# Ten sums of squares: the halves of the columns added by VectorE, and one product with ones in place of two

## What is computed

```python
def rms_norm(x, w):
    xf = x.astype(jnp.float32)
    y = xf * lax.rsqrt(jnp.mean(xf * xf, axis=-1, keepdims=True) + EPS)
    return (y * w.astype(jnp.float32)).astype(x.dtype)
```

## Time and profile before

| | |
|---|---|
| time, median of 3 runs | 2177.81 us (2176.87 to 2178.8) |
| the profiled execution, its own time | 2178.8 us |
| its span, from the first to the last instruction | 2177.1 us |
| mean granted TensorE clock, as a share of full speed | 0.997 |
| busy: TensorE, VectorE, ScalarE, GpSimd | 98%, 53%, 33%, 54% of the span |

### The profile page before, as it was taken

One profiled execution on the slowest core, in us unless ns is written; L12 is line 12 of the kernel. 1 busy time (PEld: TensorE's weight loads), 2 busy tenths in 40 slices (PEclk: granted clock), 3 DMA queues, 4 the chain that ended last, 5 costly groups with the idle time before them and its releaser, 6 DMA issues.

```text
span 2177.1 us, 29202 instructions
## 1 busy us (share of the span) xinstructions
PE 2141.7 (98%) x11096; PEld 1742.0 (80%) x11096; DVE 1150.1 (53%) x1413; ACT 710.9 (33%) x878; POOL 1180.9 (54%) x1096
## 2 busy tenths in 40 slices
PE   7999999999999999999999999999999999999997
PEld 5788887887777878777888888887888888888886
DVE  7988874367553261271389145735673334434207
ACT  6663333335533142121123241234532222212112
POOL 3342223566652232232486244466678888867776
PEclk9999999999999999999999999999999999999998
DMA  5324414232331111111323244443754455445343
GB/s 216 106 97 170 169 66 147 77 107 79 129 123 39 59 50 58 68 39 68 97 99 124 92 140 145 144 146 126 260 213 154 154 202 174 154 165 192 127 155 126
DMA packets 93601, 275.16 MB, mean 126 GB/s; under 512 B 8512, under 2 KB 19008, under 8 KB 93504
## 3 DMA queue, kind: packets, MB, share of 16 engines
q1 hardware_dynamic: 81152, 254.97, 34.0%
q10 hardware_dynamic: 12352, 18.88, 2.3%
HBM read 221.38 MB, written 52.43 MB: 126 GB/s over the span
## 4 chain that ended last, share of the span: by engine, by line
PE 89%; DVE 5%; ACT 2%; DVEq 1%; DMA 1%; POOLq 1%; issue 1%; POOL 0%; ACTq 0%; SPq 0%
PE PG L825 39%; PE PG L831 19%; PE PG L1412 14%; PE PG L1326 6%; PE PX L825 2%; PE PX L831 1%; PE PX L1055 1%; PE PX L1050 1%; DVE PX L2226 1%; PE PG L926 1%; DVE WK L2220 1%; PE PX L1033 1%; PE PX L1070 1%; PE PX L1003 0%; PE PX L1298 0%
## 5 line engine op out<-in xcount | busy, mean ns | idle before, releaser
L825 PE MATMUL PG<-UL,WH 128*128 128x512 f32 x1696 | 661.2, 390 | 0.0
L825 PE MATMUL PG<-UH,WH 128*128 128x512 f32 x1568 | 625.2, 399 | 4.5 <-ACT WK L2031 1.3
L706 POOL TENSOR_TENSOR TOUCH<-TOUCH 128x2 f32<-128x2 f32 x184 | 55.7, 302 | 828.0 <-PE PG L831 690.8
L709 POOL TENSOR_TENSOR WL<-WRAW,WH 128x1024 fp32r<-128x1024 f32 (+1 forms) x184 | 437.1, 2376 | 30.2 <-issue 30.2
L831 PE MATMUL PG<-UH,WL 128*128 128x512 f32 x1568 | 400.5, 389 | 0.0
L825 PEld LDWEIGHTS PG<-UL,WH 128*128 128x128 f32 x1696 | 318.5, 188 | 67.8 <-issue 3.8
L825 PEld LDWEIGHTS PG<-UH,WH 128*128 128x128 f32 x1568 | 294.3, 188 | 81.3 <-issue 11.2
L831 PEld LDWEIGHTS PG<-UH,WL 128*128 128x128 f32 x1568 | 294.3, 188 | 61.7
L707 POOL TENSOR_SCALAR WH<-WRAW 128x1024 fp32r<-128x1024 f32 (+1 forms) x184 | 188.8, 1026 | 0.0
L1412 PE MATMUL PG<-TH,AH 128*128 128x512 f32 x352 | 137.0, 389 | 0.3 <-POOL AL L755 0.3
L1412 PE MATMUL PG<-TH,AL 128*128 128x512 f32 x352 | 136.9, 389 | 0.0
(11 more groups left out here) (584 smaller groups left out, 3860.1 us busy)
## 6 DMA issues: line engine op xcount, KB each, us to landing
ADA<-ada_w SPq DMA_DIRECT2D x24, 1024.0 KB, 5.3
W2RAW<-down_w SPq DMA_DIRECT2D x48, 512.0 KB, 3.4
RAW<-up_w SPq DMA_DIRECT2D x22, 1024.0 KB, 6.4
WRAW<-out_w SPq DMA_DIRECT2D x30, 512.0 KB, 3.3
WRAW<-zg_w SPq DMA_DIRECT2D x24, 512.0 KB, 3.3
gates<-STG ACTq DMA_DIRECT2D x24, 512.0 KB, 2.6
WK<-gates SPq DMA_DIRECT2D x24, 512.0 KB, 3.4
WRAW<-up_w SPq DMA_DIRECT2D x22, 512.0 KB, 3.4
```

The source lines that it names most:

```text
L706: pool.tensor_tensor(TOUCH[:, 0:2], TOUCH[:, 2:4], TOUCH[:, 4:6], ALU.add)
L709: pool.tensor_tensor(WL[:, r, 0:n], WRAW[:, r, 0:n], WH[:, r, 0:n].bitcast(F32), ALU.subtract).then_inc(w_split, 1)
L825: mm = pe.matmul(out, w[:, r, at + P * k:at + P * k + P], v, start=first and k == ks[0] and n == 0, stop=False)
```

## The change

In `half_sum` one product remains, over the first 512 columns of the accumulator. VectorE's three additions go through a new helper, `square_add`: the first is as before; the second is followed by an addition of the upper half of the accumulator's columns to the lower half; the third, of 1024 columns, becomes two of 512, both into the lower half, and the semaphore is raised by the last. All ten sums are changed so. Per sum VectorE has five additions and drains in place of three.

```diff
--- before.py
+++ after.py
@@ -816,8 +816,7 @@
             def half_sum(acc, ready, count):
 
                 pe.wait_ge(ready, count)
-                pe.matmul(PX[:, SUM_BANK, :], ONES[:], WK[:, acc, 0:512], start=True, stop=False)
-                pe.matmul(PX[:, SUM_BANK, :], ONES[:], WK[:, acc, 512:1024], start=False, stop=True).then_inc(norm_ms, 1)
+                pe.matmul(PX[:, SUM_BANK, :], ONES[:], WK[:, acc, 0:512], start=True, stop=True).then_inc(norm_ms, 1)
 
             def high_products(out, r, at, ks, x, first, w=WH):
                 for k in ks:
@@ -2213,12 +2212,25 @@
 
         @block.vector
         def _(dve):
+            def square_add(u, acc, first, squares, made):
+
+                low, high = WK[:, acc, 0:512], WK[:, acc, 512:1024]
+                if u < 3:
+                    dve.tensor_tensor(WK[:, acc, :], first if u == 1 else WK[:, acc, :], squares, ALU.add).then_inc(made, 1)
+                    dve.drain()
+                if u == 2:
+                    dve.tensor_tensor(low, low, high, ALU.add)
+                    dve.drain()
+                if u == 3:
+                    dve.tensor_tensor(low, low, squares[:, 0:512], ALU.add)
+                    dve.drain()
+                    dve.tensor_tensor(low, low, squares[:, 512:1024], ALU.add).then_inc(made, 1)
+                    dve.drain()
+
             def pair_add(h, u, ready, count, acc, made):
 
                 dve.wait_ge(ready, count + 4 * h + u + 1)
-                a = y2(h, 0) if u == 1 else WK[:, acc, :]
-                dve.tensor_tensor(WK[:, acc, :], a, y2(h, u), ALU.add).then_inc(made, 1)
-                dve.drain()
+                square_add(u, acc, y2(h, 0), y2(h, u), made)
 
             def half_split(h, j0, j1, count, gain, shift=None, rs=HALF_RS):
 
@@ -2562,9 +2574,7 @@
 
             def out1_acc(h, u):
                 dve.wait_ge(post_sq, 4 * h + u + 1)
-                acc = WK[:, OUT1_ACC, :]
-                dve.tensor_tensor(acc, WK[:, 0, :] if u == 1 else acc, WK[:, u, :], ALU.add).then_inc(post_acc, 1)
-                dve.drain()
+                square_add(u, OUT1_ACC, WK[:, 0, :], WK[:, u, :], post_acc)
 
             def out1_split(h, j0, j1):
                 half_split(h, j0, j1, 16, lambda j: vec("ple_norm_w", j))
@@ -3058,9 +3068,7 @@
 
             def post_add(h, u):
                 dve.wait_ge(post_sq, 16 + 4 * h + u + 1)
-                a = WK[:, POST_SQ if u == 1 else POST_ACC, :]
-                dve.tensor_tensor(WK[:, POST_ACC, :], a, WK[:, POST_SQ + u % 3, :], ALU.add).then_inc(post_acc, 1)
-                dve.drain()
+                square_add(u, POST_ACC, WK[:, POST_SQ, :], WK[:, POST_SQ + u % 3, :], post_acc)
 
             def residual(h, u):
 
```

## The result

The changed kernel takes 2184.31 us (median of 7 runs, 2183.39 to 2185.1) against 2177.81 (median of 7, 2176.87 to 2179.11): ratio 1.003, 95% interval 1.0021 to 1.004. It is **6.5 us slower, 0.3%**. The forecast was +4.0 us (2181.8), with a range of 2177.0 to 2185.0. The profiled execution took 2183.55 us; its span is 2181.8, 4.8 us more than the span before (2177.1).

What follows compares the result with a forecast made beforehand. TensorE was taken as the bound, nine tenths of the chain that ended last. Sums 1 to 6 +3.9 and 7 to 10 -2.9 gave +1.0; the clock's +3.0 made +4.0 us, 2181.8, range 2177.0 to 2185.0.

Steps and rivals of the forecast that it cites:

- The turns: VectorE's additions alternate with GpSimd's instructions, one whole instruction each; results 3.0 us later at sum 4, 2.2 at sum 5.
- Priced by columns alone: Rival: VectorE's extra additions cost only their columns, 1.02 us per sum; -4.8 us in all, 2173.0; chance 0.12.
- The clock: TensorE's standstills at sums 4 and 5 halve its granted clock; +3.0 us together. Rival that it holds: chance 0.17.
- the fall at sum 4 costs only the sum itself: At sum 4 the low clock makes the remaining product cost 0.86 us more; the rest disappears in sum 5's wait.
- Sums 1 to 6, with the clock: First six sums: -0.86 - 0.48 + 3.0 + 2.2 = +3.9 us without the clock, and +3.0 for the clock.
- Sums 7 to 10: Last four sums: -0.76 - 0.86 - 0.86 - 0.43 = -2.9 us, each gaining from its removed product.
- Sums 1, 8 and 9 have margins of 5 us and more: Later additions stay hidden at these three sums, so each gains the full removed product, -0.86 us.
- if waits of the late sums eat their 0.86 each: Named sign that the forecast is wrong: waits at the late sums take back each one's 0.86 us gain.
- GpSimd's splits: Each split is delayed about 0.6 us by a half addition, but TensorE hardly waits for those tiles; no cost counted.
- no turn more was lost at sum 3: Rival: at sum 3 GpSimd's 706 and 707 go before the last half addition; chain 1.1 us later, +5.1; chance 0.19.
- slower by over 0.2%: Whole kernel above 2182.2 us: chance 0.35, from the lost-turn rival and a third of the forecast's case.
- the two that the prediction had priced for it: Ways to the slower outcome: a lost turn at sum 3 (+1.1 us), or a low-clock stretch twice as long (+2.1).

Runs made afterwards that it cites:

- experiment 7: Kernel before, with GpSimd's line 709 replaced by a store of zeros for 16 tiles (their low parts left out): 2175.2 us, -2.0 against before.
- experiment 8: Changed kernel with GpSimd's line 709 replaced by a store of zeros for 16 tiles: 2172.49 us, -4.75 against the kernel before.
- experiment 6: Changed kernel with 15 and 18 useless products keeping TensorE busy ahead of the waits of sums 4 and 5: 2180.2 us, +2.96 against before.
- experiment 3: Kernel before with only sums 4 and 5 in the new form: 2187.02 us, +9.45 against before.
- experiment 2: Changed kernel's additions on VectorE, but both products kept in each sum: 2189.52 us, +11.95 against before.
- experiment 5: Changed kernel with three whole additions and a single half addition behind the last: 2180.09 us, +2.85 against before.
- experiment 1: Kernel before with the second product left out of all ten sums, VectorE's additions as before: 2173.28 us, -4.3 against before.
- experiment 4: Kernel before with all sums but 4 and 5 in the new form: 2174.25 us, -3.3 against before.
- experiment 9: Kernel before with only sums 9 and 10 in the new form: 2176.84 us, -0.6 against before, no difference.
- experiment 10: Kernel before with the eight saves of H in lots of 3, 3 and 2 behind successive gate tiles: 2176.75 us, -0.7, no difference.
- experiment 11: All sums but 4 and 5 in the new form, plus the saves of H in three lots: 2172.28 us, -5.15 against the kernel before.
- experiment 12: Changed kernel with line 709 as a store of zeros for 16 tiles, plus saves of H in three lots: 2171.42 us, -6.0 against before.

## Why the prediction was right, and where it was short

**The turns: right.** The last addition of sum 4 was to end 3.87 us late; less the lead of 2.72 that is 527.53 - 2.72 = 524.81, and it ended at 524.76. For sum 5 the forecast gives 559.41 plus the 1.22 that the trace then stood at, 560.63; it ended at 560.57. The last addition of sum 7 was forecast for 1452.48; with the 5.83 that the trace then stood at that is 1458.31, and it ended at 1458.31. Experiments 7 and 8 show the cause: take line 709's reading of SBUF away and the sign of the change turns. This agrees with the rule of the Trainium skill (page SBUF — State Buffer, section Who interferes with whom) that a VectorE instruction with two SBUF inputs contends with a GpSimd instruction that reads SBUF: half additions took 1.5 to 2.7 us beside lines 707 and 709, and 0.69 beside the store. Priced by columns alone, the sum before the clock would have been -4.8.

**The clock: right in that it falls, its size in part by luck.** Both standstills, 3.59 and 4.65 us, brought a fall. Forecast +3.0; the traces of the changed kernel and of experiment 6 differ by 3.2, the medians by 3.5. The slow stretch that counts most lasted 4.7 us of TensorE's work (560.6 to 565.3), where 4.4 was taken from the first stage. That the fall at sum 4 costs only the sum itself held too: 2.12 us from the product's start to ScalarE, 1.17 in experiment 6. But the same standstills had other sizes in other traces. Behind sum 5 TensorE worked 2.9 us at the low clock in experiment 3 (561.8 to 564.7) and 3.4 in experiments 2 and 5; in experiment 3 the product of sum 4 ran at full speed.

**Sums 1 to 6, with the clock**: +6.9 forecast, +6.98 found.

**Sums 7 to 10: the step that failed.** "Sums 1, 8 and 9 have margins of 5 us and more: -0.86 each" looked at who waits for the sum's result and at whether VectorE is in time, and not at what TensorE itself issues next. Sum 9 gave 0.20: a slot of PSUM was free only when the second product would have ended. Sum 7 gave 0.75 for 0.76, sum 8 0.85 for 0.86 (with VectorE 4.42 us ahead, not 5 and more), sum 10 0.41 for 0.43. And the tile at 1554 took back 1.21. The forecast had -2.9 and should have had -1.0. The prediction had named this as a sign of being wrong ("if waits of the late sums eat their 0.86 each"), but gave it no price. "GpSimd's splits ... are for the tile after next, and TensorE hardly waits for them" is right where the loads are in time; here the tile was limited by the saves ahead of it: 17.76 us from their first issue to GpSimd's start on the tile (1539.54 to 1557.30). What TensorE gains between the two is lost, and the time itself was 0.80 longer than in the trace before. Experiments 1, 4 and 9 show the give-back at the same place. Experiments 10 to 12 show its cause: with the saves in lots the kernels that waited gain 1.8 and 1.3 us, and the kernel that did not wait shows no difference.

**The rest**, -1.30, +0.41, +1.13, +0.45 and -0.52, is +0.2 in all, so larger parts cancel. The last one is the clock ahead of the closing products (below). The others are waits elsewhere; I did not test them, and their cause stays open. That no turn more was lost at sum 3 is seen from its difference of about 0.

Sum of it: of the 2.1 us between forecast (+4.0) and trace (+6.1 from the point ahead of sum 1), 1.9 are sums 7 to 10 with their tile, and the rest is that remainder. The 6.5 us of the medians lie 0.4 above the trace's sum. The time lies inside the range, but slower by over 0.2%, which the prediction held for less likely (0.35) than no difference (0.50). And it came there by another way than the two that the prediction had priced for it: no turn was lost at sum 3, and the low clock cost only 0.2 more than forecast. That the range held is in part luck; the room left for those two was filled by the late sums.

## What to carry to other kernels

Work moved from TensorE to VectorE is not priced by columns when GpSimd reads SBUF at the same time: count the instructions, since after each one GpSimd may have a whole turn (a half addition of 0.69 us took 1.5 to 2.7 here), and look at the sums that TensorE waits for. Where TensorE has to stand still for some microseconds more, add what it loses at half clock behind the wait (3.2 us here for two waits). A gain on the busiest engine lasts only up to the next thing that comes at a time of its own (a slot emptied by another engine, a tile queued behind a burst of saves): look for waits of zero length there, and apply such a change only at the sums where it pays.

## What was not expected of the hardware

- A burst of eight 512 KB writes held the DMA share at 1.0 for some 15 us, and a tile asked for behind it came 7.8 us after its issue (1549.47 to 1557.30), where the page of the profile has 3.3 us as the median for such a tile. With the saves split into lots of 3, 3 and 2 around the tiles, the tile came in time.
- A store of zeros by GpSimd (0.95 us, it reads nothing) did not stretch VectorE's additions: beside a store alone they took 1.23 us for 128x1024 and 0.69 for 128x512 in experiment 8, and one that met line 707 first ended 0.54 us after line 707, whatever the store behind it did.
- A standstill of the same length doesn't always bring the fall at the same point of it. Ahead of the closing products TensorE stands 2.91 us in both kernels; before, the clock had fallen when they started (1.22 us), after, it was still full, which is the -0.52 at the end:

```profile
2171.34 0.70 PE L1483 MATMUL PX<-WK,ONES 128*128 128x256 f32 x2 [2.91 <-ACT WK L2190]
```

- The two falls of the changed kernel lasted 3.4 and 6.8 us, of which TensorE worked 3.0 and 4.7, behind waits of 3.59 and 4.65 us. In experiment 2 both falls began only after TensorE was back at work (0.3 and 0.6 us), and a wait of 1.60 us at sum 4 in experiment 5 brought none.
